# Up-projection products divided at columns 32 to 128, in two tiles of each of five feed-forward nets

## The reference

```
def conv_ffn(h, w_up, conv_w, conv_b, w_down):        # w_up 1024 x 5632
    u = dwconv3(h @ w_up, conv_w, conv_b)
    a, b = jnp.split(u, 2, axis=-1)
    return (jax.nn.silu(a) * b) @ w_down

def _swiglu(x, w_in, w_out):                          # w_in 1024 x 5632
    a, b = jnp.split(x @ w_in, 2, axis=-1)
    return (jax.nn.silu(a) * b) @ w_out
```

## Time and profile before

| | us |
|---|---|
| three runs | 2633.02, 2641.83, 2646.56 |
| median | 2641.83 |
| profiled execution | 2638.74 |
| its span, first to last instruction | 2636.8 |
| TensorE matmul busy | 2522.1 |
| VectorE busy | 1566.3 |
| ScalarE busy | 1224.8 |
| GpSimd busy | 190.1 |

### The profile page before, as it was taken

The page is one execution under the profiler, slowest core; times in us unless marked ns, Lnnn a source line. Parts: engine busy times, 40 slices in busy tenths (PEclk is TensorE's granted clock), DMA queues, the critical chain, the costliest instruction groups (busy, mean ns, idle before and its releaser), DMA issues.

```text
span 2636.8 us, 42072 instructions
## 1 busy us (share of the span) xinstructions
PE 2522.1 (96%) x17742; PEld 2233.1 (85%) x17742; DVE 1566.3 (59%) x2692; ACT 1224.8 (46%) x2026; POOL 190.1 (7%) x234
## 2 busy tenths in 40 slices
PE   6999999999999998989999999999999999988999
PEld 3876777776777777888889999999899999976999
DVE  2244436346655654554678876667566766766665
ACT  4235434334333334464465564455544544565543
POOL 0000000010000001000010011000100100043200
PEclk9999999999999999999999999999899999999999
DMA  7225522233434343233456546543455456531553
GB/s 252 82 96 166 170 75 86 72 112 112 147 125 158 119 155 128 88 105 119 143 178 192 192 154 209 191 147 126 142 194 192 150 193 204 169 107 36 189 192 129
DMA packets 337388, 382.13 MB, mean 145 GB/s; under 512 B 7408, under 2 KB 301296, under 8 KB 337200
## 3 DMA queue, kind: packets, MB, share of 16 engines
q1 hardware_dynamic: 334656, 370.37, 43.2%
q0 software_dynamic: 2544, 9.06, 1.1%
HBM read 378.36 MB, written 1.05 MB: 144 GB/s over the span
## 4 chain that ended last, share of the span: by engine, by line
PE 83%; ACT 7%; DVE 7%; DMA 1%; issue 1%; POOL 1%; SPq 0%; POOLq 0%; ACTq 0%; DVEq 0%
PE PS L1343 22%; PE PS L1345 22%; PE PS L1344 21%; DVE WL L2051 2%; PE PS L1380 2%; PE PS L1381 2%; PE PS L1382 2%; ACT WH L1722 1%; PE PS L1393 1%; PE PS L1483 1%; PE PS L1360 1%; POOL GT L1286 1%; DMA RAWB<-in_w_ada 1%; PE PS L1364 1%; PE PS L1458 1%
## 5 line engine op out<-in xcount | busy, mean ns | idle before, releaser
L2051 DVE TENSOR_TENSOR WL<-RAWB,WH 128x1024 fp32r<-128x1024 f32 (+2 forms) x613 | 738.1, 1210 | 515.5 <-ACT WH L1722 514.5
L1343 PE MATMUL PS<-AH,WH 128*128 128x256 f32 (+1 forms) x2912 | 908.4, 312 | 2.9 <-DVE WL L2051 2.9
L1345 PE MATMUL PS<-AH,WL 128*128 128x256 f32 (+1 forms) x2912 | 897.3, 308 | 0.0
L1344 PE MATMUL PS<-AL,WH 128*128 128x256 f32 (+1 forms) x2912 | 894.0, 307 | 0.0
L1722 ACT ACTIVATE WH<-RAWB 128x1024 fp32r<-128x1024 f32 (+2 forms) x613 | 626.2, 1033 | 285.9 <-PE PS L1345 181.2
L1343 PEld LDWEIGHTS PS<-AH,WH 128*128 128x128 f32 x2912 | 546.4, 188 | 53.9 <-issue 19.4
L1345 PEld LDWEIGHTS PS<-AH,WL 128*128 128x128 f32 x2912 | 547.3, 188 | 31.8
L1344 PEld LDWEIGHTS PS<-AL,WH 128*128 128x128 f32 x2912 | 547.1, 188 | 30.1 <-issue 0.5
L1343 PE MATMUL PS<-BH,WH 128*128 128x256 f32 (+1 forms) x1440 | 445.5, 309 | 0.8 <-DVE WL L2051 0.8
L1345 PE MATMUL PS<-BH,WL 128*128 128x256 f32 (+1 forms) x1440 | 439.3, 305 | 0.0
L1344 PE MATMUL PS<-BL,WH 128*128 128x256 f32 (+1 forms) x1440 | 437.8, 304 | 0.0
(11 more groups left out here) (312 smaller groups left out, 2715.2 us busy)
## 6 DMA issues: line engine op xcount, KB each, us to landing
RAWB<-in_f_in SPq DMA_DIRECT2D x88, 1024.0 KB, 5.1
RAWB<-in_w_in SPq DMA_DIRECT2D x52, 1024.0 KB, 5.0
RAWB<-in_w_ada SPq DMA_DIRECT2D x48, 1024.0 KB, 5.3
RAWB<-in_w_up SPq DMA_DIRECT2D x44, 1024.0 KB, 5.4
RAWB<-in_f_out SPq DMA_DIRECT2D x40, 1024.0 KB, 5.1
RAWB<-in_w_down SPq DMA_DIRECT2D x20, 1024.0 KB, 5.5
RAWB<-in_sb_qkv SPq DMA_DIRECT2D x12, 1024.0 KB, 5.1
RAWB<-in_w_out SPq DMA_DIRECT2D x8, 1024.0 KB, 5.2
```

What stands on the lines that cost most here:

```text
L1343: pe.matmul(out, h, xh[:, 0:T], start=k == 0, stop=False)
L1344: pe.matmul(out, h, xl[:, 0:T], start=False, stop=False)
L1345: i = pe.matmul(out, l, xh[:, 0:T], start=False, stop=k == g.kt - 1)
L2051: dve.tensor_tensor(c.part("WL", p), c.raw(p.slab)[:, k0:k1, c0:c1], c.part("WH", p).bitcast(F32), ALU.subtract).then_inc(up("lo", ("lo", ...
```

## The change

A table `CUT` names, for each net with 256 tokens, the third and fourth tile (part 1, hidden tiles 0 and 1) and one width for each of the 8 blocks of depth. The step `mm` carries this tuple. Where it has one, the first product of a block (high times high) is issued as two matmuls with the same stationary block: columns 0 to the width, and the width to 256. The second and third product stay whole. Only the very first matmul of a tile has `start`, as before.

```diff
+CUT = {
+    'c1': {(1, 0): (64, 64, 64, 64, 64, 64, 64, 64), (1, 1): (128, 128, 128, 128, 128, 128, 128, 128)},
+    'f10': {(1, 0): (96, 96, 96, 96, 96, 96, 96, 96), (1, 1): (112, 112, 112, 112, 112, 112, 112, 112)},
+    'f20': {(1, 0): (80, 80, 80, 80, 80, 80, 80, 80), (1, 1): (48, 48, 48, 48, 48, 48, 48, 48)},
+    'f11': {(1, 0): (32, 32, 32, 32, 32, 32, 32, 32), (1, 1): (128, 112, 100, 96, 80, 72, 64, 48)},
+    'f21': {(1, 0): (128, 112, 100, 96, 80, 72, 64, 48), (1, 1): (128, 128, 128, 128, 128, 128, 128, 128)},
+}
...
-    def __init__(self, kind, id=(), n=0, b=None, t=None, g=None, p=None, c=0, x=None):
+    def __init__(self, kind, id=(), n=0, b=None, t=None, g=None, p=None, c=0, x=None, cut=()):
+        self.cut = cut
...
-                        self.add("mm", n=n, b=b, g=g, p=p, c=0, x=True)
+                        self.add("mm", n=n, b=b, g=g, p=p, c=0, x=True, cut=CUT.get(name, {}).get((part, h0 + j), ()))
...
-                pe.matmul(out, h, xh[:, 0:T], start=k == 0, stop=False)
+                if s.cut:
+                    at_ = s.cut[k]
+                    pe.matmul(out[:, 0:at_], h, xh[:, 0:at_], start=k == 0, stop=False)
+                    pe.matmul(out[:, at_:T], h, xh[:, at_:T], start=False, stop=False)
+                else:
+                    pe.matmul(out, h, xh[:, 0:T], start=k == 0, stop=False)
                 pe.matmul(out, h, xl[:, 0:T], start=False, stop=False)
```

## The result

The changed kernel takes 2626.28 us (median of 4 runs, 2623.87 to 2629.29) against 2642.39 us for the kernel before in the same series (4 runs, 2633.02 to 2646.56): ratio 0.9949, 95% interval 0.9925 to 0.9972 (the ratio is not the quotient of the two medians, which is 0.9939). Timed again later with 12 runs it took 2626.40 us against 2638.47, ratio 0.9957 (0.9943 to 0.9972). So 80 divisions, each of which adds a matmul and a load, make the kernel 12 to 16 us faster by the medians, where I had forecast 5 us slower. The profiled execution took 2625.49 us, its span 2623.7: 13.1 us less than before.

What follows compares the result with a forecast made beforehand. TensorE, busy for 96% of the span, was taken to bound the kernel. Added time 3.30 (`f20`, `f21`) + 1.65 (`c1`) + 0.46 (`f10`) + 0 (`f11`) = 5.4 us on 2641.8 gave 2647; range 2636 to 2664, the forecast's own 2640 to 2654.

Steps and rivals of the forecast that it cites:

- a 256-column product costs 117.5 ns where TensorE runs freely: Price of one whole product on TensorE, read from eight steps in `f20` that take 0.94 us.
- +0.5, +1.65 and +1.65: Time added on TensorE in `f10` (0.46 us left after slack), `f20` and `f21` (full price, 1.65 us each).
- no mechanism: For a faster kernel it named only the runs' spread and half-clock stretches elsewhere: chance 0.04.
- The price of a division: On TensorE, two parts at 110.3 ns each replace one product of 117.5 ns: 103 ns more.
- rivals 2 and 3: Narrow fp32r parts stream at the plain fp32 rate, 2650, chance 0.10; or cost 216 ns each, 2664, chance 0.08.
- rival 4: The clock falls to half in the changed tiles, one 3.4 us stretch in each net: 2655, chance 0.05.
- my slack: In `f10`, TensorE's wait for VectorE near 1575 us hides 1.19 of 1.65 us, so 0.46 is left.
- the sixth group: In `f11`, the group of products whose tile VectorE takes at 2095.47 us, in the chain that ends TensorE's wait.
- the cover: In `f11`, 1.79 us of slack in TensorE's wait for VectorE hides the 1.65 us whole: 0 added.
- the number: In `c1`, the wait behind the tiles moves with TensorE's own tile, so the full price is added: 1.65 us.

Runs made afterwards that it cites:

- the first experiment: Against the changed kernel, only `f20` keeps its divisions (80 and 48 columns), the four other nets go undivided: 2636.8 us, ratio 0.9983 to the kernel before.
- all at 80: Against the changed kernel, both tiles of all five nets divided at 80 columns in every block: 2644.16 us, ratio 1.0018 to the kernel before.
- the last kernel: Against the changed kernel, `c1` and `f11` instead divided in six blocks at 128 of h block 6, behind their waits: 2620.79 us, ratio 0.9932 to before.

## Why the prediction was wrong

- The step that failed: "a 256-column product costs 117.5 ns where TensorE runs freely". I took that as one price for every product of that width. It is one of two paces that this product runs at, 113.3 and 117.8 ns, and the divided blocks just ahead can change which of them holds for the next 170 us. The change moves three nets to the other pace: -4.5, -4.7 and -4.9 us with the divisions already paid, where I had +0.5, +1.65 and +1.65. Both paces stood in the trace of before; I read one stretch of eight steps and let it stand for all. No rival covered it, and for faster I had "no mechanism".
- The price of a division was right. I had 103 ns; a block takes 459 to 461 ns at the old pace against 353, so 107, and 453 against 340 at the fast one, 113. It is alike at a = 80, 96, 112, 128 and 176, which rules out rivals 2 and 3; the clock is 1.00 in every stretch that shows the two paces, so rival 4 is not what moved the time either. A half-clock stretch did reach the first changed block of `f10`, but it came in the undivided `f10` of the first experiment as well, and it costs time: with the same 16 divisions `f10` takes 186.29 us with it and 184.90 without. Where the pace stays, `f20` and `f21` pay 1.72 and 1.71 us (all at 80), where I had 1.65. The shape of it was not as I said: the narrow part is followed after its own streaming (0.04 us at 80 columns), and the part behind it and the next product take the delay.
- `f10`: my slack was right where the clock is as before: all at 80, the wait is gone and the net pays 0.34 us, where I had 0.46. After the change itself the wait is gone too, but there the half-clock start alone would have removed it. What I did not see is that such a wait can turn the pace of all that follows.
- `f11`: wrong by 1 us. TensorE goes from its wait on GpSimd to the start of the wait for VectorE in 27.97 us in place of 26.36, 1.61 more where I had added 1.65, but the end of the wait moved 1.0 us too (from the net's marker, 2090.81 - 2061.53 = 29.28 against 2098.70 - 2070.43 = 28.27), and the idle time fell only from 1.63 to 1.03 us. I had followed the chain back only to the sixth group. Followed further, it begins at the fourth tile, the last changed one. VectorE took this tile at 2077.94 before, straight behind its own work (7.51 us from the marker), and stands idle for TensorE until 2070.03 after (8.50 us), so part of the cover went:

```profile
2077.94 0.41 DVE L2268 TENSOR_TENSOR Y<-Y,PS 128x256 f32<-128x256 f32 x1
...
2070.03 0.42 DVE L2281 TENSOR_TENSOR Y<-Y,PS 128x256 f32<-128x256 f32 x1 [0.93 <-PE PS L1358]
```

- `c1`: the number was right by luck. The wait stayed (1.00 us after, 0.82 before), and the stage grew by 1.49 us for 1.65. But 0.72 of that is the half-clock stretch ahead of the tiles, and only about 0.8 the divisions: 228 products between the tiles and the wait were already at the fast pace, 1.0 us less. Where the pace stays (all at 80), the net grew by 2.40 us with 0.70 of half clock in it: 1.70, the price that I gave it.

What stays open: what in the engine tells the two paces apart. The experiments show that the pace is held through unbroken runs of up to 1582 products, that divisions move it, and that behind a group of divisions it was that of the group's last block. Waits can turn it, and in `f11` it also turned without a wait where products with swapped operands begin (before at 2152.8 us from slow to fast, in the last kernel at 2135.7 us from fast to slow). They don't show the mechanism, nor why six blocks at 128 left `f20` slow in one kernel and fast in another.

## What to carry to other kernels

Where an engine's stream is uniform and fills the span, look at the steps between its instructions as a histogram, not at one mean: 4.4 ns on a step of 118 is 3.8%. If there are two heaps, see where each run of steps begins; an instruction that costs 0.1 us there can be worth 6 us. Look at the granted clock of each stage before comparing it: here 0.7 us of half clock made a wrong reckoning look right. And a small win of this kind hangs on the waits that follow: check by stage that it is still there, since the total hides it.

## What the runs showed of the hardware

- 256-column fp32r products with a load for each ran at 113.3 ns or at 117.8 ns at a granted clock of 1.00, without a gap in TensorE's records, for up to 178 us (fast) and 186 us (slow) at a time. The Trainium skill (TensorE: Matmul & The Clock Gate, Back-to-back issue gap) has one figure for this width, 262 cycles, 109 ns at 2.4 GHz, in a table for a matmul by itself; both paces measured here are above it. The same section says that in a stream of loads and matmuls both set the spacing, so the prediction read its table too simply when it set it against the price of a division.
- Two products of 128 columns with a load each, in place of one of 256, cost 107 to 113 ns more, and so do 80 and 176, in either order. That fits the 110.3 ns a load of the earlier trace rows; no run varied the load alone.
- A wait of 1 us can turn the pace: in `f10` from 113.3 to 117.8 ns behind it in one kernel, while in another the net was fast on both sides of a wait of 0.97 us. What decides the outcome wasn't seen.
- After the same standstill of 2.2 us, TensorE's next 3.5 us ran at a granted clock of 1.00 in one kernel and of 0.51 in another (`f10` before and after).
